# Latent attention of a two-block kernel: turning raw exponents, and multiplying the head outputs by reciprocals laid along rows

## The reference

```python
def block(args):                       # Q_BLOCK = 128, CHUNK = 64, 8 heads
    qi, i = args
    s = jnp.einsum('bqhd,bkhd->bhqk', qi, k, preferred_element_type=jnp.float32) * scale
    q_chunk = (i * Q_BLOCK + jnp.arange(Q_BLOCK)) // CHUNK
    mask = key_chunk[None, :] <= q_chunk[:, None]
    pr = jax.nn.softmax(jnp.where(mask, s, -jnp.inf), axis=-1).astype(v.dtype)
    return jnp.einsum('bhqk,bkhd->bqhd', pr, v)
```

## Time and profile before

| what | value |
|---|---|
| median of 3 runs | 3305.93 us (3300.36 to 3306.57) |
| the profiled execution: its own time | 3297.07 us |
| its span in the profile | 3295.4 us |
| TensorE busy over the span | 2932.7 us (89%) |
| VectorE, ScalarE, GpSimd busy | 2069.8, 1462.0, 486.3 us |
| mean granted TensorE clock | 0.945 of full |
| latent attention in the span | 371.7 to 567.65 us |

### The profile page before, as it was taken

The page is one execution under the profiler, slowest core; times in us unless marked ns, Lnnn a source line. Parts: engine busy times, 40 slices in busy tenths (PEclk is TensorE's granted clock), DMA queues, the critical chain, the costliest instruction groups (busy, mean ns, idle before and its releaser), DMA issues. The chain is left out here.

```text
span 3295.4 us, 37209 instructions
## 1 busy us (share of the span) xinstructions
PE 2932.7 (89%) x13708; PEld 2261.1 (69%) x13708; DVE 2069.8 (63%) x1976; ACT 1462.0 (44%) x1555; POOL 486.3 (15%) x495
## 2 busy tenths in 40 slices
PE   5999877999996959999997979998998849999993
PEld 3884345767664738888886757887776638888883
DVE  4888465121214668888885653234775578888884
ACT  3112444111111127778774441113664237777773
POOL 0004400000000001111111211004733200000002
PEclk8999899999997969999998989999999869999996
DMA  6112420011106256897314321110003459999995
GB/s 249 45 38 70 128 58 37 38 63 42 70 6 256 84 219 235 344 416 288 135 57 166 122 83 39 48 42 1 27 1 140 179 202 386 401 397 394 400 383 202
DMA packets 113974, 534.65 MB, mean 162 GB/s; under 512 B 15728, under 2 KB 27760, under 8 KB 74048
## 3 DMA queue, kind: packets, MB, share of 16 engines
q1 hardware_dynamic: 93904, 462.53, 36.7%
q0 software_dynamic: 15840, 57.68, 5.3%
q10 hardware_dynamic: 4112, 12.85, 1.0%
HBM read 561.47 MB, written 65.91 MB: 190 GB/s over the span
## 5 line engine op out<-in xcount | busy, mean ns | idle before, releaser
L1763 DVE TENSOR_TENSOR upper_split<-arena,upper_split 128x2048 fp32r<-128x2048 f32 x186 | 415.2, 2286 | 63.3 <-ACT upper_split L1709 63.3
L3122 DVE TENSOR_TENSOR upper_split_experts<-arena,upper_split_experts 128x2048 fp32r<-128x2048 f32 x144 | 328.9, 2292 | 45.9 <-ACT upper_split_experts L3076 44.3
L1709 ACT ACTIVATE upper_split<-arena 128x2048 fp32r<-128x2048 f32 x186 | 342.6, 1914 | 5.2 <-PE banks L177 3.9
L3076 ACT ACTIVATE upper_split_experts<-arena 128x2048 fp32r<-128x2048 f32 x144 | 275.4, 1918 | 95.2 <-PE banks L177 95.2
L175 PE MATMUL banks<-upper_split_experts 128*128 128x512 f32 x768 | 305.0, 397 | 13.2 <-DVE upper_split_experts L3122 13.2
L175 PE MATMUL banks<-upper_split 128*128 128x512 f32 x744 | 296.9, 399 | 11.7 <-DVE upper_split L1763 11.1
L177 PE MATMUL banks<-upper_split_experts 128*128 128x512 f32 x768 | 302.0, 393 | 0.0
L176 PE MATMUL banks<-upper_split_experts 128*128 128x512 f32 x768 | 301.8, 393 | 0.0
L177 PE MATMUL banks<-upper_split 128*128 128x512 f32 x744 | 291.7, 392 | 0.0
L176 PE MATMUL banks<-upper_split 128*128 128x512 f32 x744 | 291.6, 392 | 0.0
L1134 DVE TENSOR_TENSOR upper_latent<-arena,banks 128x512 f32<-128x512 f32 x48 | 33.0, 687 | 340.6 <-PE banks L1079 339.7
(11 more groups left out here) (445 smaller groups left out, 6177.6 us busy)
## 6 DMA issues: line engine op xcount, KB each, us to landing
arena<-in_exp_up_k SPq DMA_DIRECT2D x124, 1024.0 KB
arena<-in_gate_up SPq DMA_DIRECT2D x96, 1024.0 KB, 8.5
arena<-in_exp_down_k SPq DMA_DIRECT2D x62, 1024.0 KB
arena<-in_down SPq DMA_DIRECT2D x48, 1024.0 KB, 7.3
upper_middle<-in_gate_up SPq DMA_DIRECT2D x32, 1024.0 KB, 8.4
upper_middle<-in_down SPq DMA_DIRECT2D x16, 1024.0 KB, 7.1
y<-arena POOLq DMA_DIRECT2D x31, 512.0 KB, 2.9
arena<-in_merge_w SPq DMA_DIRECT2D x8, 1536.0 KB, 7.6
```

Of the source, the lines that this page charges most:

```text
L1709: a.activation(rounded(high[s]), raw[s], ACT.Copy).then_inc(high_made[up], 1)
L1763: v.tensor_tensor(rounded(low[s]), raw[s], plain(high[s]), ALU.subtract).then_inc(low_made[up], 1)
L3076: a.activation(rounded(high[n % RING]), raw[n % RAW], ACT.Copy).then_inc(high_made, 1)
L3122: v.tensor_tensor(rounded(low[n % RING]), raw[n % RAW], plain(high[n % RING]), ALU.subtract).then_inc(low_made, 1)
```

## The change

The exponents are no longer divided by their sums before they are turned: `turn(g)` waits for `exp(g)` itself. The 128x64 sums of each head are multiplied afterwards. For this the reciprocals, of which there is one per query along the partitions, have to lie along the free dimension: VectorE writes the two heads' reciprocals 64 times each beside one another (`widen`, 128x128), TensorE multiplies that with the identity (`flip`, into bank 7), ScalarE copies the result to SBUF (`lay`), and `keep` becomes a multiplication of bank 6 with it. So `sums` has one bank instead of two, and waits for the `keep` just before. On TensorE, `scores(g + 2)` now stands ahead of `turn(g)`, and `flip` and `sums` of a pair stand one step later, behind `turn` of the next pair's first step. On VectorE, `widen` of a pair stands behind `bias` of the first step two pairs on. On ScalarE, `lay` stands ahead of `move`. The row sums get four places instead of two.

```diff
             def turn(g):
-                pe.wait_ge(normed, g + 1)
+                pe.wait_ge(exped, g + 1)
                 if g:
                     pe.wait_ge(moved, g)
...
+            def flip(x):
+                pe.wait_ge(spread, x + 1)
+                if x:
+                    pe.wait_ge(flat, x)
+                pe.matmul(ps[:, 7, 0:P], wide, core.col("ident"), start=True, stop=True)\
+                  .then_inc(flipped, 1)
+
             def sums(x):
                 pe.wait_ge(moved, 2 * x + 2)
-                if x >= 2:
-                    pe.wait_ge(kept, x - 1)
+                if x:
+                    pe.wait_ge(kept, x)
...
             scores(0)
             scores(1)
             for g in range(G):
-                turn(g)
                 if g + 2 < G:
                     scores(g + 2)
-                if g % 2:
-                    sums(g // 2)
+                turn(g)
+                if g % 2 == 0 and g:
+                    flip(g // 2 - 1)
+                    sums(g // 2 - 1)
+            flip(G // 2 - 1)
+            sums(G // 2 - 1)
...
-            def normalise(g):
-                v.wait_ge(exped, g + 1)
-                c.step(v.reciprocal(rec[:, j:j + 1], den[:, j:j + 1]))
-                row = e[j][:, 0:(i + 1) * P]
-                v.tensor_scalar(row, row, rec[:, j:j + 1], None, ALU.mult).then_inc(normed, 1)
+            def widen(x):
+                here = rec[:, 2 * (x % 2):2 * (x % 2) + 2]
+                v.wait_ge(exped, 2 * x + 2)
+                if x:
+                    v.wait_ge(flipped, x)
+                c.step(v.reciprocal(here, den[:, 2 * (x % 2):2 * (x % 2) + 2]))
+                v.tensor_copy(wide.rearrange("p (j d) -> p j d", j=2),
+                              here.unsqueeze(2).to_broadcast([P, 2, 64])).then_inc(spread, 1)
 
             def keep(x):
                 v.wait_ge(summed, x + 1)
-                v.tensor_copy(oT[:, it, i * P:(i + 1) * P], ps[:, 6 + x % 2, 0:P]).then_inc(kept, 1)
+                v.wait_ge(flat, x + 1)
+                v.tensor_tensor(oT[:, it, i * P:(i + 1) * P], ps[:, 6, 0:P], rows,
+                                ALU.mult).then_inc(kept, 1)
 
             bias(0)
             bias(1)
-            normalise(0)
             for g in range(G):
-                if g + 1 < G:
-                    normalise(g + 1)
                 if g + 2 < G:
                     bias(g + 2)
                 if g % 2 == 0 and g:
+                    widen(g // 2 - 1)
+                if g % 2 == 1 and g >= 3:
                     keep(g // 2 - 1)
+            widen(G // 2 - 1)
             keep(G // 2 - 1)
...
+            def lay(x):
+                a.wait_ge(flipped, x + 1)
+                if x:
+                    a.wait_ge(kept, x)
+                a.activation(rows, ps[:, 7, 0:P], ACT.Copy).then_inc(flat, 1)
+
             exp(0)
             for g in range(G):
                 if g + 1 < G:
                     exp(g + 1)
+                if g % 2 == 0 and g:
+                    lay(g // 2 - 1)
                 move(g)
+            lay(G // 2 - 1)
```

More of the change, by code:

```diff
@@ L856, in latent_attention @@
     v_loaded = [sem(f"v{t}") for t in range(NT)]
-    scored, biased, exped, normed, turned, moved, summed, kept, steps, h_high, h_low = map(sem, (
-        "scored", "biased", "exped", "normed", "turned", "moved", "summed", "kept", "steps", "h_high", "h_low"))
+    scored, biased, exped, spread, flipped, flat, turned, moved, summed, kept, steps, h_high, h_low = map(sem, (
+        "scored", "biased", "exped", "spread", "flipped", "flat", "turned", "moved", "summed", "kept", "steps",
+        "h_high", "h_low"))
     at = UPPER + 4 * S
@@ L861, in latent_attention @@
     tiny = core.place(at + 2 * S, 16)
+    wide, rows = m["wide"], m["root_rows"]
     pt = [core.place(m["free"] + i * S, NT, P) for i in range(2)]
@@ L927, in sums @@
                         h = 2 * it + j
-                        ins = pe.matmul(ps[64 * j:64 * j + 64, 6 + x % 2, 0:P], vt[:, t, h * VH:(h + 1) * VH],
+                        ins = pe.matmul(ps[64 * j:64 * j + 64, 6, 0:P], vt[:, t, h * VH:(h + 1) * VH],
                                         pt[j][:, t, :], start=(t == 0), stop=(t == i), skip_group_check=True)
@@ L951, in bias @@
                 v.tensor_scalar(nb[:, j:j + 1], mx[:, j:j + 1], -scale, None, ALU.mult).then_inc(biased, 1)
-            def normalise(g):
-                _, i, j = where(g)
-                v.wait_ge(exped, g + 1)
-                c.step(v.reciprocal(rec[:, j:j + 1], den[:, j:j + 1]))
-                row = e[j][:, 0:(i + 1) * P]
-                v.tensor_scalar(row, row, rec[:, j:j + 1], None, ALU.mult).then_inc(normed, 1)
+            def widen(x):
[6 more added lines that the diff above has]
+                              here.unsqueeze(2).to_broadcast([P, 2, 64])).then_inc(spread, 1)
             def keep(x):
@@ L980, in exp @@
                 _, i, j = where(g)
+                x = 2 * (g // 2 % 2) + j
                 a.wait_ge(biased, g + 1)
@@ L983, in exp @@
                     a.wait_ge(turned, g - 1)
+                if g >= 4:
+                    a.wait_ge(spread, g // 2 - 1)
                 a.activation(e[j][:, 0:(i + 1) * P], flat2(ps, 2 * j)[:, 0:(i + 1) * P], ACT.Exp,
-                             bias=nb[:, j:j + 1], scale=scale, accum_out=den[:, j:j + 1]).then_inc(exped, 1)
+                             bias=nb[:, j:j + 1], scale=scale, accum_out=den[:, x:x + 1]).then_inc(exped, 1)
             def move(g):
@@ L3282, in build @@
             m["vt"] = core.place(at(45440), NT, HALF)
+            m["wide"] = core.place(UPPER + 6 * S + 16, P)
+            m["root_rows"] = core.place(at(16448), P)
             run(latent_attention, m)
```

## The result

The changed kernel took 3318.23 us (median of 6 runs, 3313.80 to 3326.13) against 3303.24 for the kernel before in the same calls (6 runs): a ratio of 1.0049, 95% interval 1.0032 to 1.0066. It is slower, by 15.0 us; the forecast was 3317, in a range of 3300 to 3325. Its profiled execution took 3314.99 us with a span of 3313.3, and a granted clock of 0.943 over the span.

The account below looks back on a forecast made before the run. A chain across engines bounds the stage: ScalarE's exponent waits for VectorE's bias, its reciprocal for the exponent. Stage +8.6 us, +11.2 with GpSimd waits, makes 3297.07 into 3308.3; with 8.9 to the median, 3317, range 3300 to 3325.

Parts of the forecast that it names:

- The stall: On TensorE, the flip waits for VectorE's copy behind a later pair's bias: some 31 times 1.2 us, 37 us in total.
- The periods: Attention stage: pairs of steps between scores' weight loads take 4.17 to 8.42 us, summing to 49.1 against 46.10 before.
- the term "0.35": On TensorE, products behind the flip can start 0.35 us after it; bounds 0.25 and 0.50.
- Chain B: Path over TensorE from the flip through sums, scores and turns: 1.85 + 0.56n + 0.22l + 0.11m, the longer from n = 5.
- A: Path over ScalarE from the flip through sums, move and exp: 2.38 + 0.45n + 0.22l + 0.11m; 5.25 us for 1 tile.
- The two periods at the change of heads: Where tiles go from 8 to 1: they took 6.39 and 2.84 us, and the new order loses 2.4 there.
- The first pair of heads: Stage's start, at half clock up to about 393: periods from 2.7 to 8.4 us, ending at 425.7 without waits for GpSimd.
- the waits for GpSimd: Early in the stage, VectorE's copy waits about 1 us for GpSimd each of three times: 2.6 us in all.
- The sum: Attention stage ends at 576.3 against 567.65 before: +8.6 us, or +11.2 with the waits for GpSimd.
- "No change": Rival: TensorE reaches full clock one or two periods sooner, 5 us back; about 3309 with TensorE's gaps at nothing; chance 0.25.
- "Faster": Rival: a late turn covers the flip's wait; 36.5 us for a pair of heads, 3268 in all; chance 0.10.
- "Much slower": Rival: half clock lasts two more periods as TensorE idles before each flip, +9 us, 3326 in all; chance 0.07.

Follow-up runs that it names:

- experiment 1: The changed kernel with widen of a pair ahead of bias(g + 2) on VectorE: 3276.58 us, ratio 0.9927 to the kernel before.
- experiment 9: The changed kernel with reciprocals written to PSUM bank 7 and copied from there: 3321.49 us, ratio 1.0064 to the kernel before.
- experiment 8: The changed kernel with turn(g) ahead of scores(g + 2) again on TensorE: 3407.78 us, ratio 1.0319 to the kernel before.
- 3: The kernel before with only scores(g + 2) moved ahead of turn(g) on TensorE: 3305.16 us, ratio 1.0006.
- 4: The kernel before with scores(g + 2) ahead of turn(g) and bias(g + 2) ahead of normalise(g + 1): 3297.86 us, ratio 0.9993.
- 5: The kernel before with scores ahead of turn, bias ahead of normalise, and sums behind the next pair's first turn: 3283.07 us, ratio 0.9943.
- 6: The kernel before with only the sums of a pair moved into the next pair's first step: 3301.26 us, ratio 0.9998.
- 7: The changed kernel with flip and sums one step later on TensorE, behind the next scores: 3314.61 us, ratio 1.0035 to the kernel before.
- experiment 2: The changed kernel with each flip issued twice, into different columns of bank 7: 3325.50 us, ratio 1.0072 to the kernel before.

## Why the prediction was right, and its sizes

**The stall.** Right in place and in total: "some 31 times 1.2 us, 37 us in total" was 30 waits and 37.9 us, and experiment 1 took it away by moving nothing but `widen`. The single waits were not all 1.2, and that the total fits so well is in part luck. In a full pair of heads the weight load of the flip waits 1.40 to 1.52 us behind scores of 3 to 8 tiles, and only 0.20 and 0.37 behind those of 1 and 2, where the prediction has about 0.9 for 1 tile.

**The periods** of a pair of steps, as the prediction has them. Forecast for n = 2 to 8, then 1: 5.15, 4.17, 4.95, 5.75, 6.64, 7.53, 8.42, 6.50. Measured between the scores' weight loads of the second pair of heads: 5.23, 4.26, 5.03, 5.82, 6.62, 7.51, 8.40, 6.63. Those of 2 to 5 tiles were each 0.07 to 0.09 short, which is the term "0.35" from flip to sums. It measured 0.42 (453.49 to 453.90 above is 0.41), nearer the 0.50 at which nothing overlaps; over 32 flips that is 2.2 us. Chain B was 0.02 long at 6 to 8 tiles, so its gaps were taken slightly too large. The estimate put on top of A for 1 tile was 0.13 short. The two periods at the change of heads, 11.86 together, lose 2.6 us against before, for 2.4 forecast. The copy took 0.23 for 0.24.

**The first pair of heads.** Forecast 56.6 us with the waits for GpSimd, measured 57.62. Three copies met GpSimd, as said, but their 0.2, 0.16 and 0.96 over 0.23 come to 1.3 us, not the 2.6 of the sum. And the clock, which rose near 394, did not stay up. The changed kernel's windows there:

```profile
394.00:396.00 2.00, 0.46 (x3) 0.06 (x1) 1.93 (x4) 0.00 (x0) 2.00 (x1) 0.92 0.00 0
396.00:398.00 2.00, 1.79 (x15) 1.23 (x16) 0.16 (x1) 0.66 (x2) 1.92 (x3) 0.94 0.00 0
398.00:400.00 2.00, 2.00 (x7) 1.31 (x6) 0.22 (x2) 0.99 (x3) 1.49 (x1) 0.50 0.00 0
400.00:402.00 2.00, 2.00 (x7) 1.18 (x6) 1.08 (x3) 1.37 (x3) 0.00 (x0) 0.71 0.62 154
```

TensorE stood idle for most of 394 to 396, and from 398 to 400 was back at 0.50, the 1.2 GHz level. In experiment 9 the copy was on time, and the clock was 0.98 from 392 to 394 and 1.00 from there to 432. By the clocks of these rows 3.4 us from 396 on ran at half clock, which is up to 1.7 us more time. The sum had 1.3 us too much for the copies and nothing for these 1.7: the two nearly cancel, and some 0.6 of the 1.0 us by which the pair of heads was missed stay unassigned.

**The sum.** The forecast was +11.2 us for the stage, and +13.96 came. The misses are +1.0 in the first pair of heads, +0.8 over the two full ones (49.5 for 49.1) and +0.9 in the last with its tail (53.3 for 52.4), together 2.7. The median moved by 15.0 us for the forecast's 11.1. That 3317 lies only 1.2 us from the 3318.23 measured is luck: the change was 3.9 us too small, and the median before that it was added to, 3305.93 of three runs, was 2.7 us above the 3303.24 of the six runs of the comparison. The stage ended at 582.1 for the "near 578" of the prediction, whose sum gives 578.9.

**The rivals.** "No change" needed the clock to rise one or two periods before 393: it didn't. "Faster" needed `wide` ready before the turn ends. Experiment 1 makes just that condition true, and its 40.4 us a pair of heads stand between the 36.5 given for it and the 46.1 before. So the mechanism was real, it was judged rightly not to hold in this order, and its size was 4 us too good. "Much slower" did not happen to the changed kernel beyond the 3.4 us above, but its mechanism, idle time before each flip and a lower clock with it, is what experiment 8 ran into.

**Where my expectations failed.** Twice, in 3 and 4, I took one wait that the trace names for the bound and expected its removal to pay. The stage has a cycle through all three engines, and as long as the sums stood right behind the turn whose move they need, the repair of VectorE's order was given back there. Of the combinations run, only `bias` first, scores first and sums later together gained (5); the scores alone (3), the sums alone (6), and scores with bias (4) each moved nothing. In 8 I left out the clock: 3335 to 3355 was expected and 3407.78 came. In 9 I counted a gain at full clock in the first pair of heads, which came, and no loss in the last, where the profiled execution had one. In 7 the time came out and the period did not.

## What to carry to other kernels

When a new step is put into a queue, ask what it needs and what the instruction ahead of it needs: a step ready early, queued behind one that waits for later data, delays its consumers by that later wait, even on the least busy engine. In a cycle over several engines, give every edit of the order its own run and then the combination; here the change's new arithmetic was worth 0.4 us in a full pair of heads of 40 (more only beside GpSimd, in the first), and the place of one statement 9. Look at the granted clock of a stretch before its length is taken for the price of an edit: in experiment 3 it would have hidden a gain of 0.3 us behind a loss of 2.3, and in experiment 8 about half of the loss came with it.

## What was not expected of the hardware

- The granted clock fell back to 0.50 behind an idle stretch on TensorE (its weight loads idle for 2.15 us) right after rising, and in experiment 8, with stretches of 1.65 to 3.09 us at every flip, it averaged 0.77. With 1.40 to 1.52 (once 1.82) at most flips the changed kernel kept 1.00 from 430 to 582 us, but experiment 9, whose order is the same, fell to 0.50 in its last pair of heads. In experiments 3 to 7 the later pairs of heads had such spells too, 3.4 to 14 us long. What brings them on was not settled.
- A copy of 128x128 within SBUF took 0.39 to 1.19 us beside GpSimd in the changed kernel, up to 2.38 in experiment 2, and 0.23 alone, while one that reads a bank took 0.29 in both cases.
- A stationary operand that reads one column 64 times over needs no copy in SBUF: the kernel that has it is the fastest, at 39.9 us a period.
